# Delta-rule scan: entry decays as rows spread by transfers, a turn's order changed, squares' sums in two rounded parts

## What is computed

```python
qkv = silu(dwconv1d_centred(proj[..., :GDN_QKV], conv_w))
q = repeat(l2_normalize(q) * GDN_HEAD_K ** -0.5, rep)      # 8 heads of 128, each used by 2 value heads
k = repeat(l2_normalize(k), rep)
g = -exp(a_log) * softplus(a_raw + dt_bias)                # per token, direction and head (16)
# per chunk and head:
gc = cumsum(g)
a_mat = (k * beta) @ k.T * exp(where(strict, seg, -inf))   # seg = gc[:, None] - gc[None, :]
sol = triangular_solve(I + a_mat, [v * beta, k * beta * exp(gc)])
q_dec = q * exp(gc)                                        # the entry decay
v_new = u - w @ S
o = q_dec @ S + (q @ k.T * exp(where(incl, seg, -inf))) @ v_new
S = exp(gc_last) * S + (k * exp(gc_last - gc)).T @ v_new
```

## Time and profile before

| | |
|---|---|
| median of 3 runs | 1656.65 us (1656.08 to 1659.39) |
| profiled execution | 1661.76 us, its span 1660.0 us |
| busy in the span | PE 1558.4 us (94%), DVE 871.9 (53%), ACT 785.0 (47%), POOL 908.9 (55%) |
| chain that ended last, by engine | PE 71%, issue 10%, ACT 6%, DVE 6%, POOL 4%, DMA 1% |

### The profile page before, as it was taken

One profiled execution on the slowest core, in us unless ns is written; L12 is line 12 of the kernel. 1 busy time (PEld: TensorE's weight loads), 2 busy tenths in 40 slices (PEclk: granted clock), 3 DMA queues, 4 the chain that ended last, 5 costly groups with the idle time before them and its releaser, 6 DMA issues.

```text
span 1660.0 us, 31033 instructions
## 1 busy us (share of the span) xinstructions
PE 1558.4 (94%) x11823; PEld 1477.5 (89%) x11823; DVE 871.9 (53%) x1804; ACT 785.0 (47%) x1395; POOL 908.9 (55%) x516
## 2 busy tenths in 40 slices
PE   4999998999998999999899999989879999999997
PEld 2899997777898999999899989878778989999996
DVE  0633203666446777613733457679775256777423
ACT  1654435766335544423755563645544255544323
POOL 1455556676572555556245556767744544555552
PEclk8999999999999999999899999999988999999998
DMA  9334446887551344434133332000002343334430
GB/s 327 103 115 126 127 126 228 289 287 264 161 157 54 125 126 126 144 127 148 50 129 104 100 102 77 15 27 27 2 27 107 123 127 90 126 126 131 140 122 38
DMA packets 55411, 205.39 MB, mean 124 GB/s; under 512 B 6145, under 2 KB 6145, under 8 KB 54913
## 3 DMA queue, kind: packets, MB, share of 16 engines
q1 hardware_dynamic: 54144, 201.70, 37.5%
q10 hardware_dynamic: 1152, 2.10, 0.4%
HBM read 196.44 MB, written 7.34 MB: 123 GB/s over the span
## 4 chain that ended last, share of the span: by engine, by line
PE 71%; issue 10%; ACT 6%; DVE 6%; POOL 4%; DMA 1%; POOLq 0%; DVEq 0%; SPq 0%; ACTq 0%
PE ps L754 6%; PE ps L756 6%; PE ps L755 6%; PE ps L662 6%; PE ps L664 5%; PE ps L663 5%; PE ps L997 4%; PE ps L998 4%; PE ps L999 4%; PE ps L2635 3%; PE ps L2637 3%; PE ps L2636 3%; POOL wlo L318 3%; ACT seg_lo L1163 2%; PE ps L388 1%
## 5 line engine op out<-in xcount | busy, mean ns | idle before, releaser
L318 POOL TENSOR_TENSOR wlo<-raw,whi 128x1024 fp32r<-128x1024 f32 (+1 forms) x195 | 494.0, 2534 | 448.7 <-ACT whi L306 448.4
L306 ACT ACTIVATE whi<-raw 128x1024 fp32r<-128x1024 f32 (+1 forms) x241 | 265.7, 1103 | 536.8 <-PE ps L664 187.9
L754 PE MATMUL ps<-hhi,whi 128*128 128x384 f32 x656 | 219.8, 335 | 2.5 <-POOL wlo L318 2.0
L828 DVE SCALAR_TENSOR_TENSOR evac<-ps,vec,evac 128x189 f32<-128x189 f32 (+3 forms) x440 | 166.5, 412 | 101.3 <-ACT evac L769 70.3
L756 PE MATMUL ps<-hhi,wlo 128*128 128x384 f32 x656 | 219.2, 334 | 0.0
L755 PE MATMUL ps<-hlo,whi 128*128 128x384 f32 x656 | 219.1, 334 | 0.0
L2419 POOL TENSOR_TENSOR wlo<-raw,whi 128x1024 fp32r<-128x1024 f32 x46 | 111.5, 2423 | 130.1 <-ACT whi L306 130.1
L997 PE MATMUL ps<-hhi,whi 128*128 128x384 f32 x392 | 133.4, 340 | 10.6 <-DVE hlo L450 9.9
L2635 PE MATMUL ps<-hhi,whi 128*128 128x384 f32 x368 | 131.0, 356 | 3.3 <-POOL wlo L2419 3.3
L999 PE MATMUL ps<-hhi,wlo 128*128 128x384 f32 x392 | 132.1, 337 | 0.0
L998 PE MATMUL ps<-hlo,whi 128*128 128x384 f32 x392 | 132.1, 337 | 0.0
(11 more groups left out here) (342 smaller groups left out, 3531.5 us busy)
## 6 DMA issues: line engine op xcount, KB each, us to landing
raw<-w_in_in SPq DMA_DIRECT2D x98, 512.0 KB, 3.6
raw<-w_ada_in SPq DMA_DIRECT2D x96, 512.0 KB, 4.6
raw<-w_up_in SPq DMA_DIRECT2D x88, 512.0 KB, 3.6
raw<-w_down_in SPq DMA_DIRECT2D x32, 704.0 KB, 4.1
raw<-w_out_in SPq DMA_DIRECT2D x32, 512.0 KB, 3.7
s<-s_ssd_in SPq DMA_DIRECT2D x8, 256.0 KB, 4.7
o_ssd_out<-st_sb ACTq DMA_DIRECT2D x8, 256.0 KB, 2.1
S<-s_gdn_in SPq DMA_DIRECT2D x4, 512.0 KB, 3.6
```

The source lines that it names most:

```text
L306: act.activation(whi[:, z.mod(SPL), 0:p.kt * P], raw[:, b.mod(RAW), 0:p.kt * P], ACT.Copy).then_inc(hi_ready, 1)
L318: pool.tensor_tensor(wlo[:, z.mod(SPL), 0:p.kt * P], raw[:, b.mod(RAW), 0:p.kt * P], whi[:, z.mod(SPL), 0:p.kt * P].bitcast(F32), ALU.subt ...
L754: pe.matmul(out, a, hhi[:, k, :], start=(k == 0), stop=False)
```

## The change

- **Entry decays.** `entry_decay` and `entry_exp` are gone with their semaphore. `rate_sums` gets four f32 matmuls with 32 stationary columns, which leave the running sums of LAT1 and LAT2 for both directions as rows of bank 7. ACT takes one exponential of them into `erow` (64 x 2 x 128). SP stores it in HBM (`e_keep`), and at the start of each turn loads four rows per direction and piece into `qe`, spread over 128 partitions: two transfers per turn behind that of the state.
- **Order of a turn.** PE makes `products(i+1, 2)` behind `level_128_first`, and `back(i, LAT2)` ahead of `products(i+2, 1)`. ACT copies the second block of diagonals behind two negations. POOL makes `state_keys` (and in turn 0 `row_keys`) ahead of the third `weighted_products` and `strengths`; `queries` now waits for the values of task 1 on DVE.
- **Squares.** ACT squares into PSUM, then copies the square, rounded, to `sq_hi` (fp32r); DVE subtracts it from the square into `sq_lo`; PE makes two fp32r matmuls in place of one f32 matmul.
- `rate_sums` and `sums_exp` stand one block later, and a semaphore of layer 0 is merged into another.

```diff
+        erow = put("erow", [64, 2, P], F32, at=st[0])
+        e_keep = nc.dram_tensor("e_keep", (2, 64, P), F32, kind="Internal").ap()
...
+                if i == 0:
+                    sp.wait_ge(g_ek, 16)
+                for d in range(2):
+                    n = 4 * i + 48 * d
+                    row = e_keep[:, n:n + 4, :].rearrange("c r n -> c (r n)").unsqueeze(0).to_broadcast([P, 2, 512])
+                    sp.dma_start(qe[:, :, d, :], row).then_inc(g_ee, 16)
                 if i == HG - 1:
                     sp.wait_ge(g_o5, 2 * HG)
...
                 if more:
-                    if i == 0:
-                        pe.wait_ge(g_ee, 2)
                     segments(pe, i + 1, 1)
-                    products(pe, i + 1, 2)
                 level_128_first(i, 0, 12)
                 level_128_first(i, 12, 24)
                 if more:
+                    products(pe, i + 1, 2)
                     segments(pe, i + 1, 2)
                     turned(pe, i + 1, 1)
                 level_128_second(i, 0)
                 if more:
                     turned(pe, i + 1, 2)
                 level_128_second(i, 1)
-                if i == 0:
-                    pe.wait_ge(g_kqs, 6)
-                    entry_decay(pe, 0, LAT2, 0, 4)
-                    pe.wait_ge(g_qk, 4)
-                    entry_decay(pe, 0, LAT2, 1, 5)
                 pe.wait_ge(g_fd, i + 1)
                 new_values(i, 0)
                 pe.wait_ge(g_fa, i + 1)
...
                     pe.wait_ge(g_qk, 3 * i + 4)
-                if i == 0:
-                    pe.wait_ge(g_ee, 4)
                 pe.wait_ge(g_wta, 4 * i + 1)
...
                     pe.wait_ge(g_vtok, 3 * i + 6)
-                    entry_decay(pe, i + 1, LAT1, 0, 4)
-                    entry_decay(pe, i + 1, LAT1, 1, 5)
                     key_rows(pe, i + 1, 2, 0, 0)
                 if far:
-                    pe.wait_ge(g_ee, 4 * i + 5)
                     products(pe, i + 2, 0)
-                    pe.wait_ge(g_ee, 4 * i + 6)
                     segments(pe, i + 2, 0)
+                back(i, LAT2)
+                if far:
+                    products(pe, i + 2, 1)
+                    turned(pe, i + 2, 0)
                 if more:
                     pe.wait_ge(g_ktok, i + 2)
-                    entry_decay(pe, i + 1, LAT2, 0, 3)
-                    entry_decay(pe, i + 1, LAT2, 1, 0)
-                if far:
-                    products(pe, i + 2, 1)
-                back(i, LAT2)
-                if far:
-                    turned(pe, i + 2, 0)
-                if more:
-                    pe.wait_ge(g_ee, 4 * i + 8)
                     pe.wait_ge(g_v, 3 * i + 3)
 
 
...
 
-                if more:
-                    diagonals(act, i + 1, 1)
-                if i == 0:
-                    entry_exp(act, 0, LAT2, 0, 4)
-                    entry_exp(act, 0, LAT2, 1, 5)
                 values(0)
                 negated(2)
                 negated(3)
+                if more:
+                    diagonals(act, i + 1, 1)
                 values(2)
                 negated(4)
                 negated(5)
...
                     keep_values(act, i + 1, 2, 0)
-                    entry_exp(act, i + 1, LAT1, 0, 4)
-                    entry_exp(act, i + 1, LAT1, 1, 5)
                     keep_keys(act, i + 1)
                 if far:
                     key_query(act, i + 2, 0)
-                if more:
-                    entry_exp(act, i + 1, LAT2, 0, 3)
-                    entry_exp(act, i + 1, LAT2, 1, 0)
                 if far:
                     decay_exp(act, i + 2, 0)
                     key_query(act, i + 2, 1)
...
 
             def queries(i):
-                pool.wait_ge(g_ee, 4 * i + 4)
+                pool.wait_ge(g_vnd, 3 * i + 1)
+                pool.wait_ge(g_ee, 32 * (i + 1))
                 for c in (LAT1, LAT2):
                     for d in range(2):
                         q = proj[:, 2 * i:2 * i + 2, tokens(c)]
@@ -2191,15 +2162,16 @@
                     weighted_products(pool, i + 1, 0)
                     weighted_products(pool, i + 1, 1)
                     decay_rows(pool, i + 1, 2)
+                if i == 0:
+                    row_keys(0)
+                state_keys(i)
+                if more:
                     weighted_products(pool, i + 1, 2)
                 strengths(i)
                 if more:
                     pool.wait_ge(g_o5, 2 * i + 2)
                     pool.wait_ge(g_dga, i + 1)
                     pool.memset(Dg[:, :, NM:TRI], 0.0).then_inc(g_pad, 1)
-                if i == 0:
-                    row_keys(0)
-                state_keys(i)
                 state_decay(i)
                 queries(i)
                 if more:
...
         inv_hi, inv_lo = (put(f"inv_{n}", [P, TOK], F32R, at=top_evac + a * nbytes([P, TOK], F32))
                           for n, a in (("hi", 3), ("lo", 4)))
         identr = put("identr", [P, P], F32R, at=top_evac + 5 * nbytes([P, TOK], F32))
+        sq_hi, sq_lo = (tuple(put(f"sq_{n}{q}", [P, TOK], F32R, at=top_evac + (a + q) * nbytes([P, TOK], F32))
+                              for q in range(2)) for n, a in (("hi", 6), ("lo", 3)))
+
+        def square_at(t):
...
             sp.dma_start(io["x_keep"], xr[:, :, :]).then_inc(x_kept, 16)
-            for s in range(14, N_IN):
+            for s in range(14, 24):
+                load_block(sp, gin, Idx(s))
+            sp.wait_ge(g_er, 1)
+            sp.dma_start(e_keep.rearrange("c r n -> r c n"), erow[:, :, :]).then_inc(g_ek, 16)
+            for s in range(24, N_IN):
                 load_block(sp, gin, Idx(s))
 
 
...
                 act.wait_ge(conv_silu, 2 + CONV_1 + t + 1)
+                if t == 8:
+                    act.wait_ge(dt_tok, 2)
+                if t:
+                    act.wait_ge(l_part, 2 * t)
+                act.activation(square_at(t), proj[:, t, :], ACT.Square).then_inc(l_sq, 1)
+                act.wait_ge(l_sq, t + 1)
                 act.wait_ge(l_mm, t + 1)
-                act.activation(evac[:, 6 + t % 2, :], proj[:, t, :], ACT.Square).then_inc(l_sq, 1)
+                act.activation(sq_hi[t % 2][:, :], square_at(t), ACT.Copy).then_inc(l_part, 1)
 
             def l2_root():
                 act.wait_ge(l_mm, 2 + QK_T)
...
             def sums_exp():
                 act.wait_ge(dt_cum, 2)
+                act.activation(erow[:, :, :], ps[0:64, 7, NB[1]:NB[1] + 2 * P].rearrange("p (c n) -> p c n", c=2),
+                               ACT.Exp).then_inc(g_er, 1)
...
 
+            def l2_low(t):
+                dve.wait_ge(l_part, 2 * t + 1)
+                dve.wait_ge(l_mm, t + 1)
+                dve.tensor_tensor(sq_lo[t % 2][:, :], square_at(t), sq_hi[t % 2][:, :].bitcast(F32),
+                                  ALU.subtract).then_inc(l_part, 1)
+
             def l2_scale(k):
...
             def l2_sum(t):
-                pe.wait_ge(l_sq, t + 1)
-                pe.matmul(ps[:, 4, 0:TOK], pick[:, 71 - l2_row(t):71 - l2_row(t) + P], evac[:, 6 + t % 2, :],
-                          start=(t == 0), stop=(t == QK_T - 1)).then_inc(l_mm, 1)
+                pe.wait_ge(l_part, 2 * t + 2)
+                one = pick[:, 71 - l2_row(t):71 - l2_row(t) + P]
+                pe.matmul(ps[:, 4, 0:TOK], one, sq_hi[t % 2][:, :], start=(t == 0), stop=False)
+                pe.matmul(ps[:, 4, 0:TOK], one, sq_lo[t % 2][:, :], start=False, stop=(t == QK_T - 1)).then_inc(l_mm, 1)
 
             def l2_spread(k):
                 r = l2_row(L2_ORDER[k])
...
                         pe.matmul(o[:, k * h:(k + 1) * h], mask(m), a[:, lo:hi], start=True, stop=True)
-                    mm = pe.matmul(o[:, 4 * h:6 * h], ones, a[:, 0:2 * h], start=True, stop=True)
+                    pe.matmul(o[:, 4 * h:6 * h], ones, a[:, 0:2 * h], start=True, stop=True)
+                for c in (LAT1, LAT2):
+                    for d, m in enumerate(("le", "ge")):
+                        mm = pe.matmul(ps[32 * d:32 * d + 32, 7, NB[1] + (c - 1) * P:NB[1] + c * P], tok_g[:, c, 0:32], mask(m),
+                                       tile_position=(0, 32 * d), start=True, stop=True)
                 mm.then_inc(dt_cum, 1)
 
...
                     rate_rows()
-                if s == 11:
+                if s == 12:
                     rate_sums()
                 if s == 23:
                     pe.wait_ge(l_std, 2)
...
                 if s == 48:
                     turned(pe, 1, 0)
-                    pe.wait_ge(g_td, 1)
-                    entry_decay(pe, 0, LAT1, 0, 6)
-                    entry_decay(pe, 0, LAT1, 1, 7)
 
```

36 lines of the change are left out of this document (15 added, 21 removed).

## The result

The changed kernel takes **1671.72 us** (median of 8 runs, 1668.14 to 1677.19); beside it the kernel before took 1658.87 (8 runs, 1656.08 to 1662.99). The ratio is 1.0080, 95% interval 1.0064 to 1.0097: some 13 us slower. The forecast was +2.8 us, and 1665 the end of its range.

A forecast was written before the change was run, and what follows sets the result against it. PE was taken to bound layer 1's projection, DVE the scan from elimination to turn's end, with four engines handing over between. Terms -2.9 + 2.1 + 1.1 + 2.5 = +2.8 on 1656.65 gave 1659.5 us; range 1650 to 1665.

The forecast's parts named there:

- The projection: Layer 1's input projection: shorter sums -4.5, longer wait at the start +0.7, added rate-sum matmuls +0.9; together -2.9 us.
- The ends of turns: End of turns 0, 1, 2: idle before the last gated product goes, saving 2.6, 2.6 and 1.2 us.
- Turn 0: Whole first turn: 4.8 for late F, +0.4 to the elimination, -0.5 for the root's idle, -2.6 at its end: +2.1 us.
- F's scaling is late by 4.8: Turn 0, POOL: eight key products ahead of F take 8.3 us, less 3.5 for POOL's earlier start.
- ACT's queue: Turns 1 and 2: products' copy precedes X, W and F copies; 4.8 us from products to L1781, at 21.1 against 17.5.
- Turns 1 and 2: From Ud to the elimination: L1781 3.6 later, then 0.5 more, less 0.44 for the root's idle: +3.7 us per turn.
- rival C: Start of turns 1 and 2: PE's clock stays at 1.2 GHz through level and products, 2.5 us per turn, 1664.5; chance 0.15.
- The copies: Turns 1 and 2: six DVE diagonal copies each wait 1.05 us for a POOL product, 6.3; level begins at 12.4.
- rival B: Turns 1 and 2: diagonal copies are free of POOL's keys, level starts at 10.8, 1.6 earlier per turn, 1656.3; chance 0.17.
- ACT's diagonals: Turns 1 and 2, L1781 to the elimination: second diagonals behind two negations make 11.3 us of 10.8, +0.5.
- D: Turns: DVE alone decides; moved products and free last diagonals save some 16 us, 1641, or 1650 with half; chance 0.20.
- E: Entry-decay transfers from HBM come late and queries wait, 2 us or more per turn, 1665 and up; chance 0.03.

The follow-up runs named there:

- sq_alone: The kernel before with only the squares' sums in two rounded parts put in, rates' sums one block later; 1656.2 us, ratio to before 0.9966.
- all_back: The changed kernel with PE's, POOL's and ACT's order edits undone; entry decays by transfer and squares in two parts stay; 1652.0 us, ratio to before 0.9949.
- pool_alone: all_back with only POOL's edit put in again (row and state keys ahead of F's scaling); 1651.5 us, ratio to before 0.9941.
- pool_back: The changed kernel with only POOL's order restored (row and state keys behind F's scaling); 1666.2 us, ratio to before 1.005.
- early_pool: early with POOL's edit of the change (row and state keys ahead of F's scaling); 1660.2 us, ratio to before 1.0005.
- pe_back: The changed kernel with only PE's products of the third piece moved back ahead of the first level of 128; 1658.9 us, ratio to before 0.9997.
- fill: The changed kernel with the third piece's products made once more, unused, at their old place ahead of the level; 1670.2 us, ratio to before 1.0061.
- dg_alone: all_back with only ACT's edit put in again (second diagonals behind the value copy and two negations); 1659.5 us, ratio to before 0.9991.
- dg_back: The changed kernel with only ACT's second diagonals moved back ahead of the value copy and two negations; 1664.7 us, ratio to before 1.0024.
- pe_alone: all_back with only PE's edit put in again (third piece's products behind the first level of 128); 1661.5 us, ratio to before 1.0007.
- after_warm: The changed kernel with three pairs of unused matmuls in PE's idle ahead of Ud, end of turns 0 to 2; 1672.0 us, ratio to before 1.0064.
- early_warm: early with two pairs of unused matmuls in PE's idle ahead of Ud; 1646.2 us, ratio to before 0.9905.
- early: all_back with the third piece's products for turns 1 and 2 made at the end of the turn before; 1648.3 us, ratio to before 0.9937.
- early_keys: early with POOL's state keys of turns 1 and 2 moved into its idle, behind a wait for DVE's diagonal copies; 1651.7 us, ratio to before 0.9942.

## Why the prediction was wrong

**The projection, -2.9**, was right: -3.2. The sums gave 0.28 each for the 0.30 that was counted, and the first one made PE wait 1.05 us. The low clock behind the rates' sums stood there before as well as after (granted 0.50 in both), so it cancelled. I had not looked at it: in sq_alone, where it is missing and the added matmuls too, the projection was 2.2 us shorter still.

**The ends of turns, -2.6, -2.6, -1.2**: the idle went in all three. From the lanes to Ud turns 1 and 2 lost 2.8 and 1.4. Turn 0 lost 1.9: it has a new wait of DVE for PE behind the lanes, 1.35 us, with PE's state_add at half clock ahead of it (4.37 for 24 records, 2.92 before). The 0.4 more that I took in each turn for the mean square's root was wrong: DVE still waits 0.46 and 0.47 for it in turns 0 and 1, and turn 2 never had that wait.

**Turn 0, +2.1; it was +3.9.** "F's scaling is late by 4.8": counted from the last gate tile, DVE's scaled F came 4.9 later (24.2 against 19.4). "8.6" from there to the lanes: 9.2. The 4.8 was luck in part. With all orders undone (all_back) the scaled F is late by 2.2 already (21.6), for a level in two pieces and at half clock, and POOL's edit by itself adds 2.3 (pool_alone, 23.9). pool_back showed ACT's queue and a level at half clock standing at the same place as POOL. I had no clock and no queue in this turn.

**Turns 1 and 2, front +3.7 each: this is the step that failed.** From Ud to the lanes it was +6.4 and +8.2. The walk's stations in turn 1, forecast and measured after Ud: level 12.4 and 13.0, its end 15.4 and 17.1, end of products 16.3 and 19.2, L1783 21.1 and 23.7, lanes 32.4 and 34.7. Two stations failed, and they are one step, PE at full clock through the level and the products: "products at full clock, 0.9" took 2.1, and "two groups of L1763, 3.0" took 4.1. ACT's queue, 4.8, took 4.6; from L1783 to the lanes it was 10.9 for 11.3. In turn 2 the whole level was slow, and L1783 began 24.9 after Ud, 8.0 later than before, for a forecast of 3.6.

So **rival C** is what came, in all three turns, where I had given it 0.15 and 2.5 us in two of them. Its price was the wrong kind of number. I took 2.5 of the 3.9 us that the slow matmuls themselves could lose, as if the rest lay beside something else. early_pool against pool_alone shows the whole of it on the path, 4.6 in a turn; the changed kernel against pe_back shows 5.3 and 6.6 in L1783's start, with the queue. And the reason I gave for it, a gap of 1.6 after 3.6 us of work, was measured as it stood: 1.61. The products that I had booked as "gone from there, so 10.8 is possible" had filled the stretch before the level. PE went from them straight into it (1117.11, 1118.49) and ran all of it at full clock. In turn 1 of the changed kernel the clock had come back without them and was lost again behind the pause. Of the change's cost in the turns, PE's edit alone carries 10.0 of 20.2.

**The copies** (term 6.3, rival B). "six of them wait for a POOL product each": in turns 1 and 2 none did. One copy waited out the rest of gr and all four products, and the others were free. There are also only six copies out of Ud in the rows, not eight. So the sum, 12.4 against 13.0, came out nearly right for the wrong reason. I had taken "one product each" from the 1.229 of turn 0, and in turn 0 it holds: 1.23, 1.19 and twice 1.11 behind four kkb products in a row.

The Trainium skill (SBUF — State Buffer, "Who interferes with whom") says that, between a VectorE copy in a two-port mode and a GpSimd operation, whoever issues first holds the shared ports for its whole instruction and the other is blocked. The trace agrees that the copy waits. What follows the product it waits for is seen in the rows alone: behind gr or a state-key product the next product of POOL went ahead of the waiting copy (4.64, 5.12 in turn 2, 5.56 in fill); behind a kkb product the copy went first, and the product after it took 1.16 in place of 1.04. This came out the same way in every kernel timed here, and why isn't shown. B fell with it in the changed kernel, but the edit costs little: pool_alone.

**ACT's diagonals**, "+0.5" from L1781 to the elimination: +0.2 in turn 1 against before, which looks right, and hides the cost. The last diagonals had become free, and this order gave that back: the step "DVE then waits for ACT's diagonals, and nothing comes of it" was right as a count and priced against the wrong kernel. dg_alone took 6.3 us over all_back, most of it behind the lanes by PE's wait and low clock in state_add, and dg_back 7.0 less than the changed kernel.

**D** fell: with the products moved and the last diagonals free, the kernel was slower. all_back and pool_alone lie 8.5 and 9.8 us below before, near its 1650, but without the move of products that D drew on; D's other half, the free last diagonals, is in pool_alone, and what they gave was lost behind the lanes. Its sum was off as well: the terms give -16.8, so 1640 and, with half of it, 1648. **E** fell: the transfers landed 5.9 to 8.7 us after they were issued, POOL used them some 30 us or more after that issue, and its queries waited 2.6 us in turns 0 to 2 (7.4 in turn 3) for DVE's values and never for a transfer.

**What stays open.** Why one order of work meets full clock in one turn and half in the next isn't settled; in pe_alone the starts of the level differ by 0.4 us. Nor is it settled why a waiting copy is passed over behind one kind of product and not behind another. fill and after_warm say that taking the low clock from one stretch of the changed kernel gives nothing while ACT's queue stands behind it, so how its 20.2 divide between clock and queues can't be given as two numbers. A level fed without waits and at full clock in every turn was not reached. As an estimate it is worth 3 to 7 us a turn, from the 55.1 of turn 2 in early_warm against 58.3 in all_back and 61.7 in its own turn 1.

## What to carry to other kernels

Before moving dense matmuls away from the front of a wait, ask what they do for the clock of the work behind it: 1.4 us of products were worth 4.6 there. Check as well what its consumer (here ACT's copy) then stands in front of. Making such feeding work early, in an idle stretch of the turn before, can be tried, but it takes the same matmuls away from that front: early gained over the kernel before, early_pool did not. Undo the edits of a bundle one at a time, and put each in alone: here one of three was free, two cost 10 and 6, and the bundle hid a gain of 8.5. And look for the cost behind the place that was edited: most of what ACT's edit cost lay there.

## What the hardware showed that I had not expected

- A VectorE copy of 0.35 us lasted 4.64, 5.12 and 5.56 us while GpSimd ran products in a row (gr, then four state-key products), and ended only with the last. Behind weighted products (kkb) in a row of the same shape, each copy waited for one of them only (1.10 to 1.23). With the state-key products held back until the copies were done, the first copy took 1.18, for the gr it met (early_keys).
- The granted clock had two outcomes for one order of instructions, in successive turns of one execution: 28.9 and 32.3 to the lanes in pe_alone, 61.7 and 55.1 for the turn in early_warm.
- Unused matmuls in the idle ahead of a turn held the first 96 small ones at full speed (1.71 in place of 2.61), but not the 128 by 512 ones some 4 us behind them (2.08 for two records, as without).
